# Two-block transformer kernel: gate and up weights of three more expert pairs, and the second block's first projection tiles, taken in halves over k

## The chip, the cores and the metric

The kernel runs on one core of one Trainium2 chip, in float32. The metric is the device time of one execution in microseconds (us), median of the runs. Times below without a unit are microseconds from the start of the profiled span.

## The reference

The input is one sequence of 256 tokens with 1024 features. Two blocks follow one another.

The first block adds a hybrid attention mixer, then a hierarchical mixture of experts: for every token a group of 8 experts is chosen out of 4, and two experts in it. Then it normalises. Each of the 32 experts is a gated network of width 256:

```python
hg = jnp.einsum('nd,edf->nef', t, w_gate)
hu = jnp.einsum('nd,edf->nef', t, w_up)
a = jax.nn.silu(hg) * hu * comb[:, :, None]
y = jnp.einsum('nef,efd->nd', a, w_down)
```

The second block normalises, projects to 3072 columns (`w_in_2`), runs an HGRN2 recurrence on four of the six groups of 512 columns and a convolution with an RG-LRU recurrence on the others, projects out, and ends with a gated feed-forward network of width 2816 and a last normalisation. The columns 2048 to 2559 of `w_in_2` are `lru_x`, the input of the convolution.

## The kernel before

TensorE (PE) does the matrix products, SyncE (SP) issues nearly all weight loads, on one DMA queue, in the order in which its program lists them. All waits are written by hand on semaphores.

**Expert stage.** The 32 experts are worked off as 16 teams of two (experts 2n and 2n+1 are team n). A team has six homes in turn for its weights (`HOMES = 6`, expert e lives in home e % 6): homes 0 to 3 are the slots of the tile `ring`, home 4 is `hs` (with `mixT` for the down weights), home 5 is `tok` and a part of `arena`. So a team's weights can be loaded as soon as the team three places ahead of it has used its own. Per team SP waits for `gate_up_used`, issues gate and up of both experts (`load_gate_up`, 1 MB each, 4 MB together; `load_half` at L572 gives whole matrices with 8 KB a partition, `load_quarter` at L578 gives 0.5 MB pieces with 4 KB a partition for home 5), waits for `chunk_used`, and issues the two down matrices (L599, 1 MB each, rows of 4 KB).

For team n, `next_team(n)` on PE waits for all of its gate and up weights (`weights_there`), then runs `gate_up` (L1218): eight steps over k, in each of them one product for each of the two experts, written as 16 `matmul` calls and seen as 32 instructions. It transposes the activations (L1273), then `down_joined` (L1294) waits for **both** down matrices and multiplies. Products that combine earlier teams (L1303) fill the gaps.

Team 3 (experts 6 and 7) and the last team, 15 (experts 30 and 31), are loaded by halves over k already: `load_last_halves` (L595) sends four 0.5 MB loads with k below 4 and then four with k from 4 on, and `gate_up(..., late=True)` waits for the second four only in front of k = 4. `LATE` says how many loads each weight has on its home's semaphore, and the thresholds `ARRIVED` are added up from it.

**Head of the second block.** Behind the last team's down product PE runs the last combining products (L1313), DVE adds them to the residual `xT` (L2526), and ACT writes `h_raw` in eight tiles (L1903, in the order `JOINED`). PE then makes four tiles of 128 columns out of `h_raw` and the first 512 columns of weight chunk `in2 0` (L1367). Each takes eight steps over k and one PSUM bank of four. The chunk comes in two loads from L660, columns 2048 to 2559 (2 MB) and columns 512 to 767 (1 MB), and PE waits for both in front of the first tile. Behind the second tile PE makes the sum of squares for a normalisation (L1373), behind the third another (L1376). What hangs on L1373 is a chain:

- ACT takes the root (L1908), DVE the reciprocal (L2548), and DVE then scales eight tiles of `hT` (L2551);
- DVE, in program order behind these eight, takes the four finished banks (L2556), and each such copy raises `u2_first` by one;
- PE's fifth tile (L1380) uses the first bank again, and so waits for `u2_first` to be 1, and it reads `hT` too.

```python
                def bank2():
                    u = unit2.up() - 1
                    if u >= 8:
                        pe.wait_ge(u2_taken, u - 3)
                    elif u >= 4:
                        pe.wait_ge(u2_first, u - 3)
                    return ps[:, u % 4, :]
```

Of the kernel before, what the change touches and what calls it, by code (L numbers as in the profile page):

```python
# [94 lines left out]
LATE = ([("expert", e, 4 if e % HOMES == HOMES - 1 or e in (HOMES, HOMES + 1) else 2) for e in range(EXPERTS)]  # L95
        + [("in2", c, 2) for c in range(4)]
        + [("out2", c, 1) for c in range(2)] + [("ffn", c, 2) for c in range(FFN_N)]
        + [("down", c, 1) for c in range(DOWN_N)])
NUMBER = {(kind, c): n for n, (kind, c, _) in enumerate(LATE)}
# [56 lines left out]
def build(nc, x, c, w_ada, b_ada, g_mix, w_in, b_forget, g_out_a, g_out_b, w_out, g_ffn, w_group,  # L156
# [3 lines left out]
    with ExitStack() as ctx:  # L160
# [282 lines left out]
        gu_done, silu_done, act_ready = sem("gu_done"), sem("silu_done"), sem("act_ready")  # L443
        turn_done, turn_taken, y_taken = sem("turn_done"), sem("turn_taken"), sem("y_taken")
        put_done, put_taken, last_halves = sem("put_done"), sem("put_taken"), sem("last_halves")
        w_y_done, w_comb_done = sem("w_y_done"), sem("w_comb_done")
        comb_done, comb_taken = sem("comb_done"), sem("comb_taken")
        parts_ready, h_ready = sem("parts_ready"), sem("h_ready")
# [53 lines left out]
        def _(sp):  # L502
# [77 lines left out]
            def load_gate_up(e):  # L580

                for g in range(2):
                    if e % HOMES <= SLOTS:
                        load_half(e, g)
                    else:
                        for far in range(2):
                            load_quarter(e, g, far)

            def load_last_halves(k_half):
# [50 lines left out]
            for team in range(HOMES // 2, TEAMS):  # L640
                sp.wait_ge(gate_up_used, team - HOMES // 2 + 2)
                if team == HOMES // 2:
                    load_early_halves(1)
                elif team == TEAMS - 1:
                    for k_half in range(2):
                        load_last_halves(k_half)
                else:
                    for e in (2 * team, 2 * team + 1):
                        load_gate_up(e)
                sp.wait_ge(chunk_used, 2 * (team - HOMES // 2) + 2)  # L650
                for e in (2 * team, 2 * team + 1):
                    load_down(e)
            in2 = w_in_2[0].rearrange("(k p) n -> p k n", p=P)
            for ch, parts in enumerate([[(2048, 2560), (512, 768)], [(768, 1024), (0, 512)],
                                        [(1024, 1536), (2560, 2816)], [(2816, 3072), (1536, 2048)]]):
                n = NUMBER["in2", ch]
                free(n)
                w, at = weights("in2", ch, KT, 768), 0
                for lo, hi in parts:
                    sp.dma_start(w[:, :, at:at + hi - lo], in2[:, :, lo:hi]).then_inc(arrived[(n + 2) % SLOTS], 16)  # L660
                    at += hi - lo
# [108 lines left out]
        def _(pe):  # L770
# [439 lines left out]
            def gate_up(n, u, first=False, late=False):  # L1210

                for k in range(KT):
                    if first and k in (0, FIRST_TILES):
                        pe.wait_ge(first_windows, 1 if k == 0 else 2)
                    if late and k == KT // 2:
                        last_halves_there()
                    for h in range(2):
                        last = pe.matmul(ps[WIN * h:WIN * (h + 1), 0, :].rearrange("p (g n) -> p g n", g=2),  # L1218
                                         lhsT=xw[:, u, k, :], rhs=expert_gate_up(2 * n + h, k),
                                         start=k == 0, stop=k == KT - 1)  # L1220
                    if first and k == KT // 2 - 1:
                        last.then_inc(gate_up_used, 1)
# [40 lines left out]
            def weights_there(n):  # L1263
                for e in (2 * n, 2 * n + 1):
                    pe.wait_ge(arrived[e % HOMES], ARRIVED["expert", e])

            def last_halves_there():
                pe.wait_ge(last_halves, 64)

            def turn_act(n):  # L1270

# [68 lines left out]
            def second_block():  # L1340
# [16 lines left out]
                    pe.wait_ge(u2_done, units)  # L1357
                    pe.sem_inc(chunk_used, 1)

                chunk_there("in2", 0)  # L1360
                w = weights("in2", 0, KT, 768)
                for i in range(4):
                    o = bank2()
                    for n, k in enumerate(JOINED):
                        if i == 0:
                            pe.wait_ge(raw_ready, n + 1)
                        last = pe.matmul(o[:, 0:L], lhsT=w[:, k, i * P:(i + 1) * P], rhs=h_raw[:, k, :], start=n == 0,  # L1367
                                         stop=n == KT - 1)
# [269 lines left out]
            with pe.Else():  # L1638
                gather()
                clear_banks()  # L1640
                for team in range(TEAMS):
                    weights_there(team)
                    if team == TEAMS - 1:
                        last_halves_there()
                    with pe.Fori(0, WINDOWS) as w:
                        n = w + team * WINDOWS
                        pe.wait_ge(windows_copied, n + 1)
# [1258 lines left out]
```

## Time and profile before

| | us |
|---|---|
| median of 3 runs | 767.14 |
| lowest and highest | 766.76, 767.94 |
| span of the profiled execution | 762.7 |
| PE busy in it | 730.6 (96%) |
| expert stage's last 4 teams, then second block from | 359.9 to 420.7 |

The page gives the span of the profiled execution, and no other time of it; the median stands 4.4 us above that span, which is what lies around the first and the last instruction. In the lists of the timeline each line is: start, length, engine, line of the program, operation, what it writes and reads, how many; in square brackets the idle time of the engine ahead of it and what ended it. PEld is the weight load that goes with each PE product.

### The profile page before, as it was taken

Reading aid. Unit: us, or ns where it says so; the run is one execution under the profiler, and the core shown is the slowest. Engines: PE = TensorE matmul, PEld = TensorE weight load, DVE = VectorE, ACT = ScalarE, POOL = GpSimd, SP = SyncE. Lnnn points to the kernel's source line nnn. Section 1 sums busy time; section 2 is a strip of 40 time slices with the busy share of each in tenths; the row PEclk is TensorE's granted clock in tenths of the full one; section 3 lists DMA queues with packets and bytes.
Section 4 is the critical chain, followed back from the end, with each engine's and each line's share of the span. In section 5 each row is a group of like instructions: output and inputs, shape, how many; then the busy total and the mean of one; then the engine's idle time right before and its main releaser. Section 6 shows DMA issues by size and latency. Waiting matters only on the chain.

```text
span 762.7 us, 9761 instructions
## 1 busy us (share of the span) xinstructions
PE 730.6 (96%) x3883; PEld 485.9 (64%) x3883; DVE 354.0 (46%) x798; ACT 188.0 (25%) x412; POOL 58.8 (8%) x69
## 2 busy tenths in 40 slices
PE   6999999998889999999989999999999999999996
PEld 4677778786524434343334886788888888885442
DVE  2125666785721212121121876364276656567445
ACT  5014323533511111111011338131321111111002
POOL 3033660040000000000001000000000000000000
PEclk9999999999999999999999999999999999999999
DMA  9998956956999999999999963123454645443401
GB/s 339 339 339 249 396 192 222 354 205 261 351 377 415 416 414 416 418 413 415 419 409 368 371 227 111 46 66 111 151 181 135 197 146 185 157 175 111 165 28 58
DMA packets 78250, 197.27 MB, mean 259 GB/s; under 512 B 3343, under 2 KB 38520, under 8 KB 72312
## 3 DMA queue, kind: packets, MB, share of 16 engines
q1 hardware_dynamic: 77248, 195.37, 68.6%
q10 hardware_dynamic: 664, 0.80, 0.4%
q0 software_dynamic: 288, 0.41, 0.3%
q8 instruction: 33, 0.54, 0.3%
q14 instruction: 17, 0.14, 0.1%
HBM read 195.33 MB, written 1.05 MB: 257 GB/s over the span
## 4 chain that ended last, share of the span: by engine, by line
PE 75%; SPq 10%; DMA 7%; DVE 5%; ACT 1%; issue 1%; POOL 1%; DVEq 0%; ACTq 0%
PE ps L1502 18%; PE ps L1218 9%; PE ps L777 9%; PE ps L1563 9%; PE ps L1294 5%; PE ps L903 4%; PE ps L1127 4%; SPq L572 4%; PE ps L914 2%; DMA arena<-in_w_up 2%; DMA ring<-in_w_ada 2%; SPq L578 2%; PE ps L1089 2%; PE ps L1099 2%; DMA ring<-in_w_in 2%; PE ps L1303 2%
## 5 line engine op out<-in xcount | busy, mean ns | idle before, releaser
L1218 PE MATMUL ps<-ring,arena 128*64 128x512 f32 x352 | 77.6, 593 | 3.1 <-DMA ring<-in_w_up 2.5
L903 PE MATMUL ps<-hs,ring 128*128 128x256 f32 (+1 forms) x288 | 66.2, 384 | 1.0 <-DMA ring<-in_w_in 1.0
L903 PEld LDWEIGHTS ps<-hs,ring 128*128 128x128 f32 (+1 forms) x288 | 52.7, 187 | 12.7 <-issue 3.8
L1218 PEld LDWEIGHTS ps<-ring,arena 128*64 128x64 f32 x352 | 26.3, 137 | 52.5 <-issue 52.5
L2848 DVE SCALAR_TENSOR_TENSOR arena<-arena,own_rows,ps 128x256 f32<-128x256 f32 x16 | 7.7, 480 | 106.8 <-ACT arena L1884 106.8
L777 PE MATMUL ps<-hs,ring 128*128 128x256 f32 x240 | 53.3, 381 | 0.3 <-PE ps L777 0.3
L777 PEld LDWEIGHTS ps<-hs,ring 128*128 128x128 f32 x240 | 45.2, 190 | 7.1 <-issue 0.9
L1502 PE MATMUL ps<-ring,hs 128*128 128x256 f32 x176 | 41.7, 380 | 0.9 <-DVE xT L2727 0.9
L1502 PE MATMUL ps<-ring,mixT 128*128 128x256 f32 x176 | 41.7, 380 | 0.0
L1502 PE MATMUL ps<-arena,mixT 128*128 128x256 f32 x176 | 41.6, 379 | 0.0
L1294 PE MATMUL ps<-ring,arena 128*64 128x512 f32 x176 | 40.2, 598 | 1.0 <-issue 0.5
L1218 PE MATMUL ps<-hs,arena 128*64 128x512 f32 x80 | 35.2, 592 | 2.2 <-DMA arena<-in_w_up 2.2
L1502 PEld LDWEIGHTS ps<-ring,hs 128*128 128x128 f32 x176 | 33.3, 190 | 6.1 <-issue 1.7
L1502 PEld LDWEIGHTS ps<-arena,mixT 128*128 128x128 f32 x176 | 33.4, 190 | 4.5
L1502 PEld LDWEIGHTS ps<-ring,mixT 128*128 128x128 f32 x176 | 32.6, 190 | 4.0
L1884 ACT ACTIVATE arena<-ps 128x256 f32<-128x256 f32 x16 | 6.1, 384 | 108.4 <-PE ps L1218 100.7
L1127 PE MATMUL ps<-mixT,ring 128*128 128x256 f32 x128 | 28.0, 380 | 0.1
L2690 DVE TENSOR_TENSOR arena<-ring 128x1024 f32<-128x1024 f32 x16 | 19.5, 1220 | 15.7 <-PE ps L1563 15.7
L1294 PEld LDWEIGHTS ps<-ring,arena 128*64 128x64 f32 x176 | 11.9, 136 | 23.1 <-issue 22.4
L1127 PEld LDWEIGHTS ps<-mixT,ring 128*128 128x128 f32 x128 | 24.2, 190 | 3.7 <-issue 0.5
L1218 PEld LDWEIGHTS ps<-hs,arena 128*64 128x64 f32 x80 | 10.9, 137 | 24.4 <-issue 24.4
L2856 DVE COPY arena<-ps 64x512 f32<-64x512 f32 x12 | 8.2, 683 | 36.6 <-PE ps L1294 36.6
(483 smaller groups left out, 1215.5 us busy)
## 6 DMA issues: line engine op xcount, KB each, us to landing
ring<-in_w_down SPq DMA_DIRECT2D x23, 1024.0 KB, 18.1
ring<-in_w_gate_up SPq DMA_DIRECT2D x22, 1024.0 KB, 7.2
ring<-in_w_gate SPq DMA_DIRECT2D x18, 1024.0 KB, 17.1
ring<-in_w_up SPq DMA_DIRECT2D x18, 1024.0 KB, 17.9
ring<-in_w_ada SPq DMA_DIRECT2D x5, 3072.0 KB, 12.9
ring<-in_w_down SPq DMA_DIRECT2D x5, 2048.0 KB, 8.1
ring<-in_w_in SPq DMA_DIRECT2D x9, 1024.0 KB, 17.1
ring<-in_w_ada SPq DMA_DIRECT2D x16, 512.0 KB, 9.3
```

Of the source, the lines that this page charges most:

```text
L572: sp.dma_start(dst, src[:, e, :]).then_inc(arrived[e % HOMES], 16)
L578: sp.dma_start(dst, src[:, e, D:2 * D] if far else src[:, e, 0:D]).then_inc(arrived[SLOTS + 1], 16)
L777: last = pe.matmul(o, lhsT=w_of(k), rhs=rhs_of(k), start=k == 0, stop=k == k_n - 1)
L903: last = pe.matmul(o[0:n, 0:L], lhsT=w[:, k, lo:lo + n], rhs=h[:, k, :], start=k == 0, stop=k == KT - 1)
L914: last = pe.matmul(o[:, i * n:(i + 1) * n], lhsT=hT[:, k, b * P:(b + 1) * P], rhs=w[:, k, lo:lo + n], start=k == 0, stop=k == KT - 1 and f ...
L1089: last = pe.matmul(ps[:, m // 2, (m % 2) * L:(m % 2 + 1) * L], lhsT=w[:, k, (m % 4) * P:(m % 4 + 1) * P], rhs=mixT[:, k, :], start=m % 2 = ...
L1127: last = pe.matmul(o, lhsT=w[:, k, (m % 4) * P:(m % 4 + 1) * P], rhs=mixT[:, k, :], start=last_of is None and m % 2 == 0 and k % 4 == 0, s ...
L1218: last = pe.matmul(ps[WIN * h:WIN * (h + 1), 0, :].rearrange("p (g n) -> p g n", g=2), lhsT=xw[:, u, k, :], rhs=expert_gate_up(2 * n + h, ...
L1294: last = pe.matmul(ps[WIN * half:WIN * (half + 1), 2, :], lhsT=act_turned[:, u, at:at + WIN], rhs=expert_down(2 * n + h)[:, k, lo:lo + 512 ...
L1502: last = pe.matmul(o, lhsT=tokens(k), rhs=columns(k), start=start and k == 0, stop=k == 3, skip_group_check=True)
L1563: last = pe.matmul(ps[:, DOWN_BANK[name], :], lhsT=lhsT, rhs=rhs, start=n == 0, stop=n == FT // 2 - 1, skip_group_check=True)
L2690: ve.tensor_tensor(sums[0], lo_2, lo_1, ALU.subtract).then_inc(weight_sums, 1)
```

## The change

Experts 24 to 29, which are teams 12, 13 and 14, are loaded by halves over k like team 15: eight loads of 0.5 MB (4 KB a partition) for a team, the four with k below 4 first. Before, teams 12 and 13 had four loads of 1 MB, and team 14 had two of 1 MB and four of 0.5 MB. The second halves count on semaphores of their own, for which PE waits in front of k = 4.

The chunk `in2 0` is loaded in five pieces instead of two: four of 0.5 MB for the first 512 columns, each over two steps of k, in the order in which PE takes them, and the 1 MB of columns 512 to 767 behind. PE runs the first four k steps of all four tiles, waits for the second pieces, runs the last four k steps of all four tiles, and waits for the 1 MB only then. The two sums of squares stay behind the second and the third tile, which are now behind the second half of these tiles.

```diff
+HALVED = range(24, 30)
+LATE = ([("expert", e, 2 if e in HALVED else 4 if e % HOMES == HOMES - 1 or e in (HOMES, HOMES + 1) else 2) for e in range(EXPERTS)]
+        + [("in2", c, 2 if c else 1) for c in range(4)]
...
+            def load_halves(team):
+                for k_half in range(2):
+                    at = k_half * D
+                    for e in (2 * team, 2 * team + 1):
+                        there = second_half_there[team % (HOMES // 2)] if k_half else arrived[e % HOMES]
+                        for g, src in enumerate((gate_d, up_d)):
...
+                            sp.dma_start(dst, src[:, e, at:at + D]).then_inc(there, 16)
...
+                elif 2 * team in HALVED:
+                    load_halves(team)
...
+                if ch == 0:
+                    for there, k in ((in2_first_k, 0), (in2_first_k, 4), (in2_second_k, 2), (in2_second_k, 6)):
+                        sp.dma_start(w[:, k:k + 2, 0:512], in2[:, k:k + 2, 2048:2560]).then_inc(there, 16)
+                    parts, at = parts[1:], 512
...
+                    if 2 * n in HALVED and k == KT // 2:
+                        second_halves_there(n)
...
-                chunk_there("in2", 0)
                 w = weights("in2", 0, KT, 768)
+                first_banks = [bank2() for _ in range(4)]
+                pe.wait_ge(in2_first_k, 16 + 32)
                 for i in range(4):
-                    o = bank2()
-                    for n, k in enumerate(JOINED):
+                    for n, k in enumerate(JOINED[0:4]):
                         if i == 0:
                             pe.wait_ge(raw_ready, n + 1)
...
+                pe.wait_ge(in2_second_k, 16 + 32)
+                for i in range(4):
+                    for n, k in enumerate(JOINED[4:8]):
...
                     last.then_inc(u2_done, 1)
                     if i == 1:
                         pe.wait_ge(sums_ready, SUMS["g"])
...
+                chunk_there("in2", 0)
                 o = bank2()
```

## Rows read from the trace of the kernel before

**Rows 1.** The page: span, and the first engine of its part 1.

```profile
span 762.7 us, 9761 instructions
PE 730.6 (96%) x3883; PEld 485.9 (64%) x3883; DVE 354.0 (46%) x798; ACT 188.0 (25%) x412; POOL 58.8 (8%) x69
```

**Rows 2.** Timeline of PE, teams 12 to 15 and the head of the second block.

```profile
359.89 7.09 PE L1218 MATMUL ps<-ring,arena 128*64 128x512 f32 x32 [0.67 <-DMA ring<-in_w_up]
...
374.95 7.09 PE L1218 MATMUL ps<-ring,arena 128*64 128x512 f32 x32 [1.80 <-DMA ring<-in_w_up]
...
390.16 0.61 PE L1218 MATMUL ps<-hs,arena 128*64 128x512 f32 x1 [2.16 <-DMA arena<-in_w_up]
...
403.24 7.04 PE L1218 MATMUL ps<-ring,arena 128*64 128x512 f32 x32
...
412.59 3.65 PE L1294 MATMUL ps<-ring,arena 128*64 128x512 f32 x16
...
420.75 7.17 PE L1367 MATMUL ps<-tok,ring 128*128 128x256 f32 x32 [0.52 <-DMA ring<-in_w_in]
```

**Rows 3.** The chain that ended last: team 14's last up load, issue to landing.

```profile
371.72 18.31 DMA arena<-in_w_up
```

**Rows 4.** Busy time by stretch of 5 us; last column GB/s, before it DMA share.

```profile
362.00:367.00 5.00, 5.00 (x25) 1.81 (x21) 0.00 (x0) 0.00 (x0) 0.00 (x0) 1.00 1.03 424
367.00:372.00 5.00, 5.00 (x24) 2.82 (x26) 1.68 (x7) 0.77 (x2) 0.00 (x0) 1.00 1.01 420
...
382.00:387.00 5.00, 4.94 (x27) 2.45 (x28) 1.83 (x7) 1.32 (x4) 0.00 (x0) 1.00 1.01 406
387.00:392.00 5.00, 2.84 (x16) 0.96 (x14) 0.68 (x1) 0.59 (x1) 0.00 (x0) 1.00 1.02 407
...
397.00:402.00 5.00, 5.00 (x26) 2.81 (x26) 1.68 (x7) 0.77 (x2) 0.00 (x0) 1.00 1.03 411
```

**Rows 5.** Loads at L595, one first half and the last second half: issue, landing.

```profile
L595 SPq DMA_DIRECT2D ring<-in_w_up x1: 1076/1076/1076, 384.4 to 384.4; - x1
DMA to landing us min/median/max: 15.8/15.8/15.8
...
L595 SPq DMA_DIRECT2D ring<-in_w_up x1: 3156/3156/3156, 388.4 to 388.4; - x1
DMA to landing us min/median/max: 17.0/17.0/17.0
```

**Rows 6.** Loads at L599 of experts 30 and 31, issued 391.6 and 392.7.

```profile
L599 SPq DMA_DIRECT2D ring<-in_w_down x2: 1076/1638/2200, 391.6 to 392.7; - x2
...
DMA to landing us min/median/max: 16.3/17.9/19.5
```

**Rows 7.** Loads at L660 of chunk in2 0, 2 MB and 1 MB.

```profile
L660 SPq DMA_DIRECT2D ring<-in_w_in x2: 2197/5940/9682, 395.0 to 397.2; - x2
...
DMA to landing us min/median/max: 22.8/23.1/23.5
```

**Rows 8.** Timeline of all engines, head of the second block.

```profile
419.94 3.31 ACT L1903 ACTIVATE tok<-xT,gains 128x256 f32<-128x256 f32 x8 [3.06 <-DVE xT L2526]
...
428.28 0.70 PE L1373 MATMUL ps<-arena,ones 128*128 128x256 f32 x2 [0.35 <-DVE arena L2541]
...
429.02 0.38 ACT L1908 ACTIVATE rstd<-ps 128x256 f32<-128x256 f32 x1 [2.57 <-PE ps L1373]
...
430.46 1.75 DVE L2548 RECIPROCAL rstd<-rstd 128x256 f32<-128x256 f32 x1
...
432.25 3.26 DVE L2551 SCALAR_TENSOR_TENSOR hs<-xT,gains,rstd 128x256 f32<-128x256 f32 x8
...
432.70 3.62 PE L1367 MATMUL ps<-tok,ring 128*128 128x256 f32 x16
...
435.44 0.41 DVE L2556 TENSOR_TENSOR arena<-ps,rstd 128x256 f32<-128x256 f32 x1
...
435.94 1.05 PEld L1380 LDWEIGHTS ps<-hs,ring 128*128 128x128 f32 x5
```

More of the change, by code:

```diff
@@ L94 @@
 FFN_PARTS = {"q": 1, "u": 2, "gate 1": 3, "up 1": 4, "up 0": 5}
-LATE = ([("expert", e, 4 if e % HOMES == HOMES - 1 or e in (HOMES, HOMES + 1) else 2) for e in range(EXPERTS)]
-        + [("in2", c, 2) for c in range(4)]
+HALVED = range(24, 30)
+LATE = ([("expert", e, 2 if e in HALVED else 4 if e % HOMES == HOMES - 1 or e in (HOMES, HOMES + 1) else 2) for e in range(EXPERTS)]
+        + [("in2", c, 2 if c else 1) for c in range(4)]
         + [("out2", c, 1) for c in range(2)] + [("ffn", c, 2) for c in range(FFN_N)]
@@ L445, in build @@
         put_done, put_taken, last_halves = sem("put_done"), sem("put_taken"), sem("last_halves")
+        second_half_there = (last_halves, ada0_there["scale 0"], ada0_there["scale 3"])
+        second_half_before = (0, 16 * 3, 16 * 2)
+        in2_first_k, in2_second_k = in0_first, in0_second
         w_y_done, w_comb_done = sem("w_y_done"), sem("w_comb_done")
@@ L587, in load_gate_up @@
                             load_quarter(e, g, far)
+            def load_halves(team):
[4 more added lines that the diff above has]
+                        for g, src in enumerate((gate_d, up_d)):
+                            h = e % HOMES
+                            if h < SLOTS:
+                                dst = ring[:, h, g * KT * FE + at:g * KT * FE + at + D]
+                            elif h == SLOTS:
+                                dst = hs[:, g].rearrange("p k t -> p (k t)")[:, at:at + D]
+                            else:
+                                dst = far_gate_up[:, g].rearrange("p k n -> p (k n)") if k_half else tok[:, g, :]
+                            sp.dma_start(dst, src[:, e, at:at + D]).then_inc(there, 16)
             def load_last_halves(k_half):
@@ L1265, in weights_there, with second_halves_there @@
                     pe.wait_ge(arrived[e % HOMES], ARRIVED["expert", e])
+            def second_halves_there(n):
+                i = n % (HOMES // 2)
+                teams = sum(m % (HOMES // 2) == i for m in range(HALVED[0] // 2, n + 1))
+                pe.wait_ge(second_half_there[i], second_half_before[i] + 64 * teams)
             def last_halves_there():
-                pe.wait_ge(last_halves, 64)
+                pe.wait_ge(last_halves, 128)
             def turn_act(n):
@@ L1358, in chunk2_used @@
                     pe.sem_inc(chunk_used, 1)
-                chunk_there("in2", 0)
                 w = weights("in2", 0, KT, 768)
+                first_banks = [bank2() for _ in range(4)]
+                pe.wait_ge(in2_first_k, 16 + 32)
                 for i in range(4):
-                    o = bank2()
-                    for n, k in enumerate(JOINED):
+                    for n, k in enumerate(JOINED[0:4]):
                         if i == 0:
                             pe.wait_ge(raw_ready, n + 1)
-                        last = pe.matmul(o[:, 0:L], lhsT=w[:, k, i * P:(i + 1) * P], rhs=h_raw[:, k, :], start=n == 0,
-                                         stop=n == KT - 1)
+                        pe.matmul(first_banks[i][:, 0:L], lhsT=w[:, k, i * P:(i + 1) * P], rhs=h_raw[:, k, :],
+                                  start=n == 0, stop=False)
+                pe.wait_ge(in2_second_k, 16 + 32)
+                for i in range(4):
+                    for n, k in enumerate(JOINED[4:8]):
+                        if i == 0:
+                            pe.wait_ge(raw_ready, n + 5)
+                        last = pe.matmul(first_banks[i][:, 0:L], lhsT=w[:, k, i * P:(i + 1) * P], rhs=h_raw[:, k, :],
+                                         start=False, stop=n == 3)
                     last.then_inc(u2_done, 1)
@@ L1644, in _ @@
                         last_halves_there()
+                    if 2 * team in HALVED:
+                        second_halves_there(team)
                     with pe.Fori(0, WINDOWS) as w:
```

## The prediction

> **What bounds the kernel now.** I read the page first: PE is busy for 730.6 of 762.7 us [rows 1], so a gain must come out of the few places where PE stands still, and whatever delays PE is paid in full. Then I read PE's timeline in the stretch that the change touches [rows 2]. It shows three waits for gate and up weights: 0.67 us ahead of team 12, 1.80 us ahead of team 13, 2.16 us ahead of team 14, together 4.63 us. Team 15, in halves already, starts without a wait, and the second block's first tile waits 0.52 us for its chunk. The chain that ended last runs through team 14's last load, issued at 371.7 and landed at 390.0 [rows 3]: there the DMA stream sets the pace, and not PE.
>
> The third view is the stream itself. In the stretches of 5 us it moves 406 to 424 GB/s with the DMA engines at a share of 1.01 to 1.03 [rows 4]; it is full, and SP has issued far ahead. Its order is fixed, so an earlier PE makes no byte land earlier. The fourth view, issue and landing, gives the stream's milestones: team 15's first halves are there at 384.4 + 15.8 = 400.2, its second halves at 388.4 + 17.0 = 405.4 [rows 5]; the down matrix of expert 30 at 391.6 + 16.3 = 407.9 and that of 31 at 392.7 + 19.5 = 412.2 [rows 6]; the chunk's 2 MB at 395.0 + 22.8 = 417.8 and its 1 MB at 397.2 + 23.5 = 420.7 [rows 7]. PE starts team 15's down product at 412.59 [rows 2]. So PE, which looks free of waits there, is only 0.4 us behind the stream. That is the number that decides about the expert part.
>
> **Team 12 to 14 in halves, taken alone.** A halved team can start 2 MB ahead of its last byte; 2 MB took 405.4 - 400.2 = 5.2 us [rows 5]. A team's products take 7.09 us with their tail, 7.0 us of issue, so 3.5 us a half [rows 2]. PE was ready at 359.22 for team 12, 373.15 for team 13 and 388.00 for team 14 (start less wait). Team 12 then starts at once and gains 0.67; team 13 too, and gains 0.67 + 1.80 = 2.47; team 14 starts its first half at 385.5, is through at 389.0 and waits about 1 us for the last halves. It ends some 3.5 us earlier than now. PE would like to keep these 3.5 us.
>
> **What the smaller rows cost the stream.** The change makes rows of 4 KB out of rows of 8 KB for 10 MB (4 + 4 + 2). The trace holds both kinds: while team 13's whole matrices flow, the rate is 424 and 420 GB/s, while team 14's quarters, down matrices and team 15's halves flow it is 406, 407 and 411 [rows 4]. 10 MB are 10.5e6 bytes: 24.9 us at 422 and 25.7 us at 408, so 0.8 us more. The bounds are 0, if the difference is of the place and not of the rows, and 1.0 us at the extreme pair of these rows (424 and 406 give 1.1). I take 0.8, as the rates follow the kind of load in every one of these rows. The issuing itself costs nothing: SP issues about 15 us ahead of the landing even where it sends the 0.5 MB loads [rows 5], and with thirteen more issues up to the end of this chunk (4, 4, 2, and 3 for the chunk), about 1.1 us each in these rows, it waits for a full queue, not the queue for it.
>
> At this place the Trainium skill speaks against the change: the page "DMA: Bandwidth & Descriptors" (sections "Anatomy of one DMA" and "Bandwidth") gives a fixed 2.0 us to every transfer and wants 1 MiB or more in each. By the formula, if the fixed parts stood in a row, the ten more expert loads would be 20 us; the trace shows that they overlap. The rows that say so: four loads of 0.5 MB landed within 5.2 us of each other, which is their bytes at 403 GB/s and leaves nothing like a fixed part [rows 5].
>
> **What is left of the gain.** With 0.8 us on the stream: team 14's last halves at 390.8, so team 14 ends at 394.4 instead of 397.2 and PE is ready for team 15 at 400.4 instead of 403.24. Team 15's first halves come at 401.0, its second halves at 406.2, so its gate and up end at 409.8 (now 410.3). PE is ready for the down product at 412.1, but the second down matrix lands at 412.2 + 0.8 = 413.0. So the down product starts at about 413.05, which is 0.45 us **later** than now. Nothing of the 3.5 us comes through; the wait has moved to `down_joined` of team 15, and its queue behind it is everything PE has left.
>
> **The chunk in halves.** The first tile starts now at 420.75, because of the 1 MB that it doesn't need. Without that it could start when ACT has written the first tile of `h_raw`, 419.94 + 0.41 = 420.35 [rows 8], so at about 420.4. Its 1 MB of first pieces lies ahead of the present landing at 417.8 and is there. With the 0.45 us the start is at 420.85, 0.1 us later than now.
>
> **The new order of the four tiles.** A tile takes 3.45 us (two in 7.17 with the tail) [rows 2], half a tile 1.72. Now L1373 starts 7.53 us behind the first tile's start, 0.35 of it a wait. In the new order it stands behind six halves: 10.35 us. From there the chain runs on: ACT starts 0.65 us behind (0.63 to 0.74 by how the products pile up), 0.38 for the root, 1.75 for the reciprocal, 3.2 from the first of the eight scalings to the first bank copy, 0.41 for that, 0.1 to the weight load of L1380 [rows 8]. Now the reciprocal starts 1.06 us behind the root's end, because DVE is busy adding squares; later it is free, so 0.05. Sum: 10.35 + 0.65 + 0.38 + 0.05 + 1.75 + 0.05 + 3.2 + 0.41 + 0.1 = 16.94 us from the first tile's start to the fifth tile. PE has work for 4 tiles and two small sums, 14.7 us, and then stands still for 2.3 us. Now this distance is 15.2 us to the weight load at 435.94 and 15.4 to the product, which follows the fourth tile at 432.70 + 3.45 = 436.15. The first bank is taken at 435.85, 0.1 us ahead of the load: the chain has no slack today. The new order costs 16.94 - 15.4 = 1.5 us. This is hard to escape: each term is a duration of this trace, and the one thing that moves is L1373, by 2.8 us less the 1.0 us in which DVE was busy and less the wait.
>
> **The sum.** 0.1 + 1.5 = +1.6 us at the fifth tile. Behind it PE waits almost nowhere in the second block, so the shift reaches the end. DVE's work behind L2556 moves by as much as PE's. 762.7 + 1.6 = 764.3 for the span; with the 4.4 us around it, 768.7 on the median of 767.14. The bounds: with no cost of rows +0.8, and with 1.1 us of it +1.9.
>
> **Rivals.** *The stream's tail catches up.* Expert 31's down matrix lands 4.3 us behind that of 30 though 1 MB is 2.6 us, so some engines lag by 1.7 us [rows 6]. If the shorter rows even this out, the down product starts at 412.1, the first tile at 419.9, and the fifth tile is 0.7 us later than now: 767.8. For it: the lag is not explained. Against: the chunk's own small rows follow it as before.
>
> *The gain comes through* (the other side: faster). One mechanism: the stream does run earlier at its end, so that team 15's halves and expert 31's down matrix don't hold PE, all of the 3.5 us is kept, and the first tile starts 3.4 us ahead of 420.4 at 417.0. Even then the 1.5 us of the new order are paid: 417.0 + 16.94 - 436.15 = -2.2, so 764.9. It decides from the point at which expert 31's down matrix lands ahead of 409.7 (then -1.5). Against: 2.5 us would have to come out of a full stream.
>
> *Every transfer costs a fixed time.* Ten more expert loads hold the stream one by one. By the nearest rows the fixed part is at most 5.2 us less 2 MB at 422 GB/s (4.97), over four loads, 0.06 each; that makes 0.6 us and is no more than my own term. A large one, 0.5 us a load, would give 5 us: 772.
>
> *The halves do nothing for PE,* because the loads in flight land interleaved and the first halves come with the last. Then team 14 ends at 397.9, team 15 at 411.1, the down product starts at 413.4 and the fifth tile is 2.0 us later: 769.2. Against: team 15 didn't wait at all in the kernel before.
>
> **The numbers.** My forecast, 768.7, has 0.55, the catching-up tail 0.2, the gain that comes through 0.1, the interleaved halves 0.1, a large fixed time 0.02; 0.03 is for what I don't see. A measurement of this kernel can tell about 0.2% from no change, 1.5 us. My forecast lies just above that edge, with some 0.6 us of scatter on each side: slower in 0.6 of its cases. With the interleaved halves slower is 0.47, same 0.43, faster 0.10. The range from 765.8 to 770.2 takes in both bounds, the caught-up tail, the interleaved halves and half of the faster case.
>
> **What would show each step.** PE's timeline: the waits at L1218 of teams 12 and 13 gone, one of 1 to 1.7 us inside team 14, one inside team 15, one at L1294 of team 15 until 413.0. The stretches from 350 to 385: about 410 GB/s where it was 420. L1373 some 10.4 us behind the first tile, and a wait of 2.3 us in front of L1380, ended by DVE's L2556. I am wrong if L1294 of team 15 starts ahead of 411.5, or if L1380 follows the fourth tile without a gap.

## The result: 769.03 us, 1.0024 of before

22 runs of the changed kernel have a median of 769.03 us (767.17 to 772.51), 22 runs of the kernel before 767.20 us. The ratio is 1.0024, with a 95% interval of 1.0014 to 1.0034: 1.8 us slower (1.1 to 2.6), where the prediction said 1.6 us slower and 768.7 us.

The span of the profiled execution is 767.7 us and its own time 769.48 us, so 1.8 us lie around the span. (The 4.4 us of the prediction compared the span of one quick execution of before with a median of others. It was taken off and added again, so the forecast of the median doesn't hang on it.) Against the 762.7 us of [rows 1] that is 5.0 us, more than the change is worth. A part of it stands ahead of everything that was changed. These lines are PE's timeline at team 1 in the changed kernel, then the busy time of the stretch (granted clock third from the end):

```profile
214.01 5.35 PE L1327 MATMUL ps<-ring,arena 128*64 128x512 f32 x16 [0.47 <-ACT arena L1932]
```
```profile
215.00:220.00 5.00, 5.00 (x18) 1.55 (x16) 0.60 (x1) 0.59 (x1) 0.00 (x0) 0.69 1.01 391
```

The same 16 products took 3.65 us in the kernel before. The granted clock was 0.69 on the mean of these 5 us, so about 3 us were run at 1.2 GHz instead of 2.4, and PE lost 1.7 us. No such stretch is in the profile of before while PE works. The stream came later in two steps. The second down matrix of team 8 landed at 305.9 instead of 304.5; this may be the fall of the clock, as SP's loads wait for PE up to there, but it isn't taken apart. Team 10 then needed 16.5 us on the stream instead of 15.1, with loads that were not changed and at the full clock; why stays open. Together that is 2.8 us. So traces are compared below by distances inside one trace, counted from a point that lies ahead of the change and belongs to the stream: the landing of team 11's last down matrix. The lines are issue and landing, first the kernel before, then the changed one:

```profile
L599 SPq DMA_DIRECT2D arena<-in_w_down x1: 2509/2509/2509, 329.2 to 329.2; - x1
DMA to landing us min/median/max: 20.6/20.6/20.6
```
```profile
L619 SPq DMA_DIRECT2D arena<-in_w_down x1: 2508/2508/2508, 332.0 to 332.0; - x1
DMA to landing us min/median/max: 20.6/20.6/20.6
```

That is 349.8 and 352.6. I call it the mark. Times of the changed trace have to be lowered by 2.8 us to stand beside those of before. Landings are read to 0.1 us here, so a distance from the mark is no better than that.

### The profile page after: what moved, and what is told of

Read it like the earlier page. It is cut to its first block, busy times and chain, and to the rows that moved or that the text cites. A ratio compares the mean times of both kernels' runs of the same rounds, so it can differ in the third digit from the quotient of the medians.

```text
span 767.7 us, 9775 instructions
## 1 busy us (share of the span) xinstructions
PE 732.8 (95%) x3883; PEld 485.3 (63%) x3883; DVE 355.0 (46%) x798; ACT 187.6 (24%) x412; POOL 58.6 (8%) x69
## 3 DMA queue, kind: packets, MB, share of 16 engines
HBM read 195.33 MB, written 1.05 MB: 256 GB/s over the span
## 4 chain that ended last, share of the span: by engine, by line
PE 79%; DMA 7%; SPq 6%; DVE 4%; issue 1%; POOL 1%; ACT 1%; DVEq 0%; ACTq 0%
PE ps L1543 17%; PE ps L1246 11%; PE ps L803 9%; PE ps L1604 9%; PE ps L1327 6%; PE ps L929 4%; PE ps L1153 4%; DMA ring<-in_w_down 3%; PE ps L940 2%; DMA ring<-in_w_ada 2%; PE ps L1336 2%; PE ps L1115 2%; PE ps L1125 2%; DMA ring<-in_w_in 2%; SPq L538 1%; SPq L615 1%
## 5 line engine op out<-in xcount | busy, mean ns | idle before, releaser
L1246 PE MATMUL ps<-ring,arena 128*64 128x512 f32 x352 | 77.9, 593 | 2.9 <-DMA ring<-in_w_up 2.3
L1327 PE MATMUL ps<-ring,arena 128*64 128x512 f32 x176 | 41.9, 619 | 1.9 <-DMA ring<-in_w_down 0.9
## 6 DMA issues: line engine op xcount, KB each, us to landing
ring<-in_w_in SPq DMA_DIRECT2D x9, 1024.0 KB, 15.8
```

The lines of the kernel that those rows point to most:

```text
L1327: last = pe.matmul(ps[WIN * half:WIN * (half + 1), 2, :], lhsT=act_turned[:, u, at:at + WIN], rhs=expert_down(2 * n + h)[:, k, lo:lo + 512 ...
```

## The profile after

PE's timeline of the changed kernel, teams 13 to 15 and the second block's head, beside [rows 2]:

```profile
378.20 3.65 PE L1246 MATMUL ps<-ring,arena 128*64 128x512 f32 x16 [0.42 <-DMA ring<-in_w_up]
...
388.53 0.61 PE L1246 MATMUL ps<-hs,arena 128*64 128x512 f32 x1 [0.69 <-DMA tok<-in_w_up]
...
393.50 0.64 PE L1246 MATMUL ps<-hs,arena 128*64 128x512 f32 x1 [1.32 <-DMA arena<-in_w_up]
...
403.83 3.65 PE L1246 MATMUL ps<-ring,arena 128*64 128x512 f32 x16 [0.51 <-DMA ring<-in_w_up]
...
408.85 3.65 PE L1246 MATMUL ps<-ring,arena 128*64 128x512 f32 x16 [1.37 <-DMA ring<-in_w_up]
...
415.80 3.65 PE L1327 MATMUL ps<-ring,arena 128*64 128x512 f32 x16 [0.89 <-DMA ring<-in_w_down]
...
423.80 7.14 PE L1400 MATMUL ps<-tok,ring 128*128 128x256 f32 x32 [0.36 <-ACT tok L1946]
...
440.77 3.69 PE L1421 MATMUL ps<-hs,ring 128*128 128x256 f32 x16 [2.06 <-issue]
```

The three waits of before, 4.63 us, have become six: 0.42 inside team 13, 0.69 and 1.32 at the two halves of team 14, 0.51 and 1.37 at those of team 15, 0.89 ahead of its down product. Together 5.20 us: what was gained ahead of team 14 is waited for behind it. The first tile starts 71.20 us behind the mark, before it was 420.75 - 349.8 = 70.95. And a new wait of 2.06 us stands in front of L1421, the fifth tile.

The stream, in the same stretches as [rows 4] and two between (last column GB/s):

```profile
362.00:367.00 5.00, 5.00 (x26) 1.72 (x24) 0.05 (x1) 0.00 (x0) 0.00 (x0) 1.00 1.02 408
367.00:372.00 5.00, 5.00 (x24) 2.62 (x22) 1.67 (x7) 0.77 (x2) 0.00 (x0) 1.00 1.03 410
372.00:377.00 5.00, 5.00 (x26) 1.72 (x24) 0.68 (x1) 0.59 (x1) 0.00 (x0) 1.00 1.03 408
377.00:382.00 5.00, 4.58 (x22) 1.28 (x19) 0.00 (x0) 0.01 (x1) 0.00 (x0) 1.00 1.03 411
```

The stretches of 420 and 424 GB/s are gone; all run at 408 to 411. Two things have changed in these loads, the length of their rows and their number, and the landings tell the two apart. These are the last load of gate and up weights of team 13, first in the kernel before (1 MB, rows of 8 KB), then in the changed one (0.5 MB, rows of 4 KB):

```profile
L572 SPq DMA_DIRECT2D ring<-in_w_up x1: 2118/2118/2118, 351.7 to 351.7; - x1
DMA to landing us min/median/max: 23.1/23.1/23.1
```
```profile
L607 SPq DMA_DIRECT2D ring<-in_w_up x1: 1222/1222/1222, 362.2 to 362.2; - x1
DMA to landing us min/median/max: 16.0/16.0/16.0
```

They land at 374.8 and 378.2. The second down matrix of the team ahead had landed at 364.9 and 367.9, that of team 13 itself lands at 379.9 and 383.3. So before, 4 MB in rows of 8 KB took 9.94 us (to the hundredth in the trace) and the 2 MB of down matrices, two loads of 1 MB in rows of 4 KB, took 5.11 us. In the changed kernel the 4 MB took 10.23 us in pieces of 0.5 MB, and the down matrices 5.13. With rows of 4 KB a MB costs 2.56 us, in loads of 1 MB and of 0.5 MB alike; with rows of 8 KB it costs 2.49. The number of transfers costs nothing that shows here. (The down matrices are another tensor; that difference is left.)

Issue and landing at the end of the stream, beside [rows 5] (last second half of team 15) and [rows 6] (the down matrices of experts 30 and 31):

```profile
L615 SPq DMA_DIRECT2D ring<-in_w_up x1: 1241/1241/1241, 393.5 to 393.5; - x1
DMA to landing us min/median/max: 15.3/15.3/15.3
...
L619 SPq DMA_DIRECT2D ring<-in_w_down x2: 1089/1640/2190, 394.8 to 395.9; - x2
...
DMA to landing us min/median/max: 18.3/19.0/19.8
```

They land at 408.8, 413.1 and 415.7. Behind the mark that is 56.2, 60.5 and 63.1 us; before, 405.4, 407.9 and 412.2 less 349.8 are 55.6, 58.1 and 62.4. So the matrix that PE waits for is 0.7 us later.

The head of the second block, all engines, beside [rows 8]:

```profile
434.24 0.59 PE L1413 MATMUL ps<-arena,ones 128*128 128x256 f32 x2
...
434.87 0.38 ACT L1951 ACTIVATE rstd<-ps 128x256 f32<-128x256 f32 x1 [5.23 <-PE ps L1413]
435.29 1.75 DVE L2591 RECIPROCAL rstd<-rstd 128x256 f32<-128x256 f32 x1 [1.54 <-ACT rstd L1951]
...
437.07 3.25 DVE L2594 SCALAR_TENSOR_TENSOR hs<-xT,gains,rstd 128x256 f32<-128x256 f32 x8
...
440.27 0.41 DVE L2599 TENSOR_TENSOR arena<-ps,rstd 128x256 f32<-128x256 f32 x1
...
440.74 3.32 PEld L1421 LDWEIGHTS ps<-hs,ring 128*128 128x128 f32 x16 [2.43 <-issue]
```

The sum of squares stands 10.44 us behind the first tile instead of 7.53. DVE is idle when the root is done, the reciprocal follows at once, the eight scalings, then the copy of the first bank, whose end at 440.68 releases the fifth tile. PE's own work was done 2.06 us ahead of the fifth tile's start.

## The experiments

In the table the first tile is counted from the mark (in the same trace), and the seventh tile (the one that starts behind a gap of 0.30 us in every one of these kernels) from the first tile. Both are read in one profiled execution each; the ratio is of many runs. It isn't the quotient of the medians, from which it differs by up to 0.6 us in these experiments.

The last column is an estimate from the runs' times and mean clocks. The 103 executions of before that stand beside the experiments, in three sets, show how time goes with the clock: a line through them, each set around its own mean, gives 0.60 us more for every thousandth of mean granted clock less, and it takes up 0.65 of the variance. The column is the mean of a kernel's runs less the mean of before beside them, brought to the same clock by that line, in us, with two standard errors of the means. For the change itself the clocks of before are not on record. What the clock does is taken up in the last section.

| kernel | ratio to before, 95% | first tile | seventh tile | sum | at equal clock, us |
|---|---|---|---|---|---|
| before | 1 | 70.95 | 22.78 | 93.73 | 0 |
| the change | 1.0024 (1.0014 to 1.0034) | 71.20 | 24.43 | 95.63 | - |
| experts only | 0.9989 (0.9976 to 1.0002) | 71.67 | 22.58 | 94.25 | +0.1 ± 0.4 |
| chunk only | 1.0022 (1.0010 to 1.0035) | 70.86 | 24.43 | 95.29 | +1.2 ± 0.5 |
| sum early | 1.0003 (0.9991 to 1.0016) | 71.17 | 22.93 | 94.10 | 0.0 ± 0.6 |
| rows only | 1.0023 (1.0011 to 1.0036) | 73.21 | 22.92 | 96.13 | +0.4 ± 0.7 |
| more rows | 1.0025 (1.0009 to 1.0041) | 71.15 | 24.42 | 95.57 | +2.1 ± 0.7 |
| split down | 1.0003 (0.9986 to 1.0019) | 70.46 | 24.43 | 94.89 | +0.4 ± 0.6 |
| old order, late 1 MB | 0.9994 (0.9978 to 1.0010) | 70.80 | 22.92 | 93.72 | 0.0 ± 0.4 |
| filled waits | 0.9971 (0.9956 to 0.9986) | 70.79 | 22.93 | 93.72 | -0.5 ± 0.4 |
| all together | 0.9985 (0.9975 to 0.9995) | 70.27 | 22.93 | 93.20 | -0.5 ± 0.5 |
| fifth tile's wait filled | 1.0033 (1.0020 to 1.0047) | 71.09 | 24.42 | 95.51 | +2.1 ± 1.0 |
| team 14 alone, filled | 0.9995 (0.9984 to 1.0005) | 69.75 | 22.93 | 92.68 | -0.9 ± 0.6 |
| filled waits, late 1 MB | 1.0012 (0.9999 to 1.0026) | 70.82 | 22.93 | 93.75 | +0.2 ± 0.8 |

The ratios stray from the traces' sums by up to 2.2 us (0.7 in the middle). At equal clock nine of the twelve experiments agree with their trace within the two errors, if 1.7 us are taken off "rows only" for a fall of the clock in its own profile; "experts only" and "filled waits" miss by little, "split down" by 0.8 us.

**Experts only.** The chunk `in2 0` as before.

```diff
-        + [("in2", c, 2 if c else 1) for c in range(4)]
+        + [("in2", c, 2) for c in range(4)]
...
-                if ch == 0:
-                    for there, k in ((in2_first_k, 0), ...
...
+                chunk_there("in2", 0)
                 for i in range(4):
-                    for n, k in enumerate(JOINED[0:4]):
+                    for n, k in enumerate(JOINED):
```

> Experts 24 to 29 in halves as in the changed kernel; the chunk in2 0 is loaded, waited for and used as before. My theory: the stream comes 0.8 us later from the 4 KB rows, PE's 3.5 us are taken away by the waits of team 15, and the chunk's 1 MB lands at 421.5 instead of 420.7, so +0.8 us against before (768.0). L1373 stands 7.5 us behind the first tile, no wait in front of the fifth tile. Rival, the gain of PE comes through: -0.3 us or better. Rival, the expert halves cost what the whole change costs: +1.9 us.

Its timeline of PE from team 14's second half on:

```profile
391.13 0.64 PE L1242 MATMUL ps<-hs,arena 128*64 128x512 f32 x1 [1.35 <-DMA arena<-in_w_up]
...
406.50 3.65 PE L1242 MATMUL ps<-ring,arena 128*64 128x512 f32 x16 [1.38 <-DMA ring<-in_w_up]
...
413.50 3.65 PE L1323 MATMUL ps<-ring,arena 128*64 128x512 f32 x16 [0.97 <-DMA ring<-in_w_down]
...
421.86 7.17 PE L1396 MATMUL ps<-tok,ring 128*128 128x256 f32 x32 [0.71 <-DMA ring<-in_w_in]
...
429.19 0.70 PE L1402 MATMUL ps<-arena,ones 128*128 128x256 f32 x2 [0.16 <-DVE arena L2572]
```

In the trace everything is where I had put it: the mark is at 350.2, the first tile 0.7 us later than before, waiting for the chunk's 1 MB at the end of a stream that is 0.7 us late. The seventh tile is 0.5 us late, since the wait for the sum shrank. But the runs are 0.9 us faster than before by the ratio (from 1.8 faster to 0.2 slower) and 0.55 us by the medians, where I had said 0.8 slower. Their mean clock was higher, 0.9976 against 0.9966; at equal clock 0.1 us slower is left. "Rows only" and the section on the clock take this up.

**Chunk only.** The experts as before (`HALVED = range(0, 0)`), the rest of the change kept.

> No expert in halves beyond those of before; the chunk in2 0 in five pieces and the four tiles in the new order, as in the changed kernel. My theory: the first tile starts 0.3 us earlier (420.4), the sum of squares stands 10.35 us behind it instead of 7.5, the fifth tile 16.9 us behind it instead of 15.4: +1.2 us against before (768.4). PE waits 2 to 2.3 us in front of the fifth tile. Rival, the order costs nothing because the waits are hidden: -0.3 us.

```profile
423.01 7.15 PE L1400 MATMUL ps<-tok,ring 128*128 128x256 f32 x32 [0.36 <-ACT tok L1946]
...
439.99 3.69 PE L1421 MATMUL ps<-hs,ring 128*128 128x256 f32 x16 [2.06 <-issue]
```

1.7 us slower by the ratio, 1.56 us by the trace, 1.2 us expected. The first tile waits for ACT and no longer for the load, but this gain is only 0.1 us behind the mark, and the new order takes 24.43 instead of 22.78 us. Nearly the whole loss of the change is in this part.

**Sum early.** The changed kernel with another order on PE, nothing else (`half_tiles(tiles, half)` runs four k steps of these tiles):

```diff
+                half_tiles((0, 1), 0)
                 pe.wait_ge(in2_second_k, 16 + 32)
                 for i in range(4):
...
+                    if i == 2:
+                        half_tiles((2, 3), 0)
+                    last = half_tiles((i,), 1)
                     last.then_inc(u2_done, 1)
                     if i == 1:
                         pe.wait_ge(sums_ready, SUMS["g"])
```

> The changed kernel, but PE takes both halves of tiles 0 and 1 first, then the sum of squares L1373, then both halves of tiles 2 and 3. All loads and waits on loads stay. My theory: the sum is back at 7.5 us behind the first tile, the fifth tile at 15.4 us, the wait of 2.1 us in front of it is gone: 1.5 us faster than the changed kernel, +0.1 to +0.4 us against before. Rival, the wait in front of the fifth tile has another cause (the chunk's 1 MB, or the code of PE): no change against the changed kernel, 1.0024 of before.

```profile
422.88 7.15 PE L1403 MATMUL ps<-tok,ring 128*128 128x256 f32 x32 [0.35 <-ACT tok L1950]
...
430.57 0.70 PE L1417 MATMUL ps<-arena,ones 128*128 128x256 f32 x2 [0.54 <-DVE arena L2588]
...
445.81 7.14 PE L803 MATMUL ps<-hs,ring 128*128 128x256 f32 x32 [0.30 <-PE ps L803]
```

The sum is 7.69 us behind the first tile, the wait in front of the fifth tile is gone, the seventh tile stands at 22.93 instead of 24.43: 1.5 us. By the ratios 1.0024 became 1.0003, 1.6 us. This shows where the change loses: in the place of L1413 in PE's program.

**Rows only.** As "experts only", but PE waits for the second halves ahead of k = 0.

```diff
-                    if 2 * n in HALVED and k == KT // 2:
+                    if 2 * n in HALVED and k == 0:
                         second_halves_there(n)
```

> As the run with only the experts in halves, but PE waits for the second halves ahead of k = 0 already, so it has the smaller rows and none of the earlier starts. My theory: PE waits 1 to 3 us in one piece in front of teams 12, 13 and 14, team 14 starts 0.8 us later than before, the down product of team 15 too, and the end is +0.8 us against before: the same as with the earlier starts, since the stream decides. Rival, the halves are worth something to PE: this run is 1 us or more slower than the one with only the experts in halves.

1.8 us slower than before by the ratio, and 2.6 us slower than "experts only"; by the medians of the same runs it is 1.2 and 1.7 us. I had expected no difference between the two. The trace gives one reason, in team 14 and in the stretch around it (granted clock third from the end):

```profile
390.84 0.64 PE L1242 MATMUL ps<-hs,arena 128*64 128x512 f32 x1 [2.25 <-DMA arena<-in_w_up]
...
391.29 1.04 PE L1242 MATMUL ps<-hs,arena 128*64 128x512 f32 x1
```
```profile
385.00:390.00 5.00, 3.59 (x17) 1.00 (x16) 1.80 (x7) 0.71 (x2) 0.00 (x0) 1.00 1.03 411
390.00:395.00 5.00, 4.16 (x12) 1.62 (x14) 0.00 (x0) 0.00 (x0) 0.00 (x0) 0.66 1.02 409
```

Behind a wait of 2.25 us the products of 593 ns take 1040: PE runs at 1.2 GHz for some 3.4 us, and team 14's products take 8.7 us instead of 7.0. Of the 2.3 us by which the first tile is late, this is 1.7; the rest, 0.6, is the late stream. The stream itself is as in "experts only": mark at 349.8, last load of team 14 40.9 us behind it (before 40.2). Without the 1.7 us the sum would be 94.4, beside 94.3 of "experts only": in the trace the earlier starts are worth nothing at the end, as expected. The difference of the runs is for the most part one of the clock, 0.9952 against 0.9976. At equal clock 0.3 us of it are left, which is within the errors.

**More rows.** Experts 18 to 29 in halves (`HALVED = range(18, 30)`).

> The changed kernel with experts 18 to 29 in halves instead of 24 to 29: 10 MB more in rows of 4 KB. My theory, the smaller rows cost the stream 0.08 us a MB: the down matrix of expert 31 lands 0.8 us later against the stream's own start than in the changed kernel, and the kernel is 0.8 us slower than the changed one (1.0034 of before). Rival, the later end of the stream has to do with the last teams alone: as the changed kernel, 1.0024.

The ratio is 1.0025, beside 1.0024 of the changed kernel; the interval (0.0016 to each side) holds both 1.0024 and the expected 1.0034. The mark lies within the changed rows here, so its sum of 95.57 lacks what teams 9 to 11 cost. Between the second down matrices of teams 8 and 9, and of 9 and 10, the stream needs 15.4 us each, where it needs 15.1 in the kernel before: 0.3 us for each team of 4 MB, as expected. Team 11 is no witness, 15.8 us against 15.2: the changed kernel shows at team 10, with whole matrices, that a single team can be later by more than that (16.5). So the cost of the rows shows in the stream, and whether it reaches the end stays open.

**Split down.** The changed kernel with a later wait:

```diff
                 for h in range(2):
                     pe.wait_ge(down_there[(2 * n + h) % HOMES], DOWN_THERE[2 * n + h])
-                for h in range(2):
                     for k in range(2):
```

> The changed kernel, but the down product waits for the second expert's down matrix only behind the first expert's products (1.8 us later), in all teams. My theory, PE's gain dies at the wait for expert 31's down matrix: team 15's down product starts 0.9 us earlier against the stream and the kernel is 0.9 us faster than the changed one (1.0012 of before). Rival, the gain is gone already at team 15's halves: no change against the changed kernel.

```profile
407.17 3.65 PE L1246 MATMUL ps<-ring,arena 128*64 128x512 f32 x16 [1.38 <-DMA ring<-in_w_up]
...
421.15 7.14 PE L1399 MATMUL ps<-tok,ring 128*128 128x256 f32 x32 [0.36 <-ACT tok L1945]
```

The wait at the down product is gone and the first tile stands 70.46 us behind the mark, 0.74 earlier than in the changed kernel (expected 0.9). The ratio went from 1.0024 to 1.0003, 1.6 us, with intervals that overlap. The place where PE's gain is lost last is this wait; the 1.38 us inside team 15 is the one ahead of it.

**Old order, late 1 MB.** The kernel before, but the chunk comes in five pieces and the 1 MB of columns 512 to 767 is waited for in front of the fifth tile only. PE's part, against the kernel before:

```diff
-                chunk_there("in2", 0)
+                pe.wait_ge(in2_first_k, 16 + 32)
+                pe.wait_ge(in2_second_k, 16 + 32)
...
+                chunk_there("in2", 0)
                 o = bank2()
```

> The kernel before, but the chunk in2 0 comes in five pieces and PE waits for the 1 MB of columns 512 to 767 only in front of the fifth tile; order of the tiles and sums and the experts' loads as before. My theory: first tile at 420.4 instead of 420.75, nothing lost behind it: -0.3 us (0.9996). Rival, the pieces themselves cost something: +0.3 us or more.

The ratio says nothing here (0.9978 to 1.0010). The trace does: the first tile is 0.15 us earlier, the seventh 0.14 us later behind it, the sum is the same 93.7. PE waits 0.54 instead of 0.35 us for the squares in front of the sum, for they depend on the experts' result and not on the tiles. So an earlier first tile wins nothing, even without the new order.

**Filled waits.** The kernel before with two products more:

```diff
                 pe.wait_ge(windows_copied, n + 1)
+                if n in (TEAMS - 3, TEAMS - 2):
+                    for _ in range(2):
+                        pe.matmul(ps[:, 0, :], lhsT=ones[:], rhs=xT[:, 0:2, :].rearrange("p k t -> p (k t)"), start=True,
+                                  stop=True)
                 weights_there(n)
```

> The kernel before with two added products of 512 columns (1.7 us, result overwritten) ahead of the wait for the weights of team 13 and of team 14, where PE stands still for 1.8 and 2.2 us. It tells whether the earlier starts are worth time through the clock. Theory A, such a standstill lets the granted clock fall to 1.2 GHz for some 3 us in a part of the executions (seen in the profile of the run with the smaller rows alone: 0.66 in 390 to 395): mean clock of the runs up by 0.001 and the median 0.5 us or more below before. Theory B, the clock has nothing to do with these waits: median +0.0 to +0.2 us, clock as before.

2.2 us faster than before (1.1 to 3.4), with the trace's distances unchanged at 93.72. The mean granted clock over the 12 runs was 0.9977, over the 35 runs of before beside them 0.9959. Both are as theory A had it, but the last experiment doesn't bear it out, and in the traces the falls of the clock stand elsewhere (see the last section).

**All together.** Experts 24 to 29 in halves, the split wait, the old order, the late 1 MB.

> The changed kernel's experts in halves, the down product waiting for its second expert only in front of that expert's products, the tile order and the sums as before, and the chunk's 1 MB waited for in front of the fifth tile. My theory: of the changed kernel's +1.9 us the new order's 1.5 us go and the wait for expert 31's down matrix goes (0.9 us); by the terms it is 0.5 us faster than before, and 1 us faster if the shorter standstills keep the clock up as in the run with the experts alone (0.9987 to 0.9993). Rival, the wait moves on to the first pieces of the chunk: no better than 1.0.

0.9985, the interval wholly below 1: 1.2 us faster than before. The trace gives 0.5 of it (93.20), as the terms had said, and so do the runs at equal clock.

**Fifth tile's wait filled.** The changed kernel with two products of 512 columns into an idle bank behind the fourth tile.

> The changed kernel with two added products of 512 columns (1.7 us, result unused) behind the fourth tile, where PE stands still for 2.06 us in front of the fifth. They can't move the fifth tile earlier. Theory A, this standstill too lets the clock fall in a part of the executions: mean clock above the changed kernel's 0.9958 and the median 0.5 us or more below the changed kernel's (1.0015 of before or less). Theory B, the whole cost of the new order is the standstill itself: 1.0024 of before, as the changed kernel.

```profile
438.83 3.69 PE L1424 MATMUL ps<-hs,ring 128*128 128x256 f32 x16 [0.34 <-issue]
```

The wait is 0.34 instead of 2.06 us, the seventh tile is where it was (24.42), and the ratio is 1.0033, not lower than 1.0024. Filling this wait brings nothing; whether the products add something can't be told from the intervals.

**Team 14 alone, filled.** Only experts 28 and 29 in halves, the split wait, the old order, the late 1 MB, and the two products ahead of team 13.

> Only experts 28 and 29 in halves (2 MB in smaller rows, 0.15 us on the stream), the later wait for the second down matrix, tile order as before, the 1 MB waited for in front of the fifth tile, and two added products in the 1.8 us wait of team 13. By the terms: team 14 ends 2.1 us earlier, team 15's second halves let 1.1 us of it through, the down product no less, the first tile at 419.3: 1.4 us faster than before from the starts, and some 0.5 us more from the clock: 0.9975 to 0.9982. Rival, it is the clock alone that counts: as the run with the added products, 0.9971, or no better than 0.9990 if team 14's shorter wait was the one that mattered.

The trace gives the best sum of all, 92.68, 1.05 us ahead of before: 1.4 had been expected, 0.3 of it from the late 1 MB, which is worth nothing. The ratio, 0.9995 (0.9984 to 1.0005), shows less, and lies outside the 0.9975 to 0.9982 that I had named; the mean clock was 0.9962, in the runs of before beside it 0.9968.

**Filled waits, late 1 MB.** The kernel before with the added products of "filled waits" and the late 1 MB of "old order".

> The kernel before with the added products ahead of the waits of teams 13 and 14 and the chunk's 1 MB waited for in front of the fifth tile: the two runs 0.9971 and 0.9994 together. If they add up 0.9965; if the first was an outlier of its session, 0.9985.

1.0012, above both values that I had named. With the added products in the same place as in "filled waits" the mean clock was 0.9959 (before beside it 0.9968), and the 0.9971 did not come back.

## Why the prediction was right, point by point

*The stream gets slower by the 4 KB rows, 0.8 us.* Held: 408 to 411 GB/s where it was 420 to 424, the last load of team 14 and expert 31's down matrix both some 0.7 us later behind the mark. "Rows only" and "experts only" show the same with the chunk left alone (team 14's last load 40.9 us behind the mark in both, against 40.2). That it is the rows, and not the number of transfers, is shown by the down matrices of 1 MB, which cost as much for each MB as the pieces of 0.5 MB. The prediction gives its upper bound once as 1.0 and once as 1.1 us; the rows give 1.1.

*PE's 3.5 us are lost to the halves and the down matrix of team 15.* Held: waits of 0.51, 1.37 and 0.89 us where the prediction's milestones give 0.6, 1.7 and 0.9. Team 15's down product starts at 415.80 less 2.8, so at 413.0, where it had 413.05. Taking the last of the waits away moved the first tile by 0.74 us.

*The first tile starts 0.1 us later.* 0.25 us: the same sum, with a small miss.

*The new order costs 1.5 us.* The fifth tile starts 440.77 - 423.80 = 16.97 us behind the first, where the chain of terms gave 16.94; PE's wait is 2.06 us where I had 2.3: the prediction counted PE's work by the starts of its products, and the wait is counted from the end of the last one. "Sum early" gives back 1.50 us. The seventh tile is 1.65 us further behind the first than before. The other 0.15 us is lost in the old order too once the first tile no longer waits for the 1 MB, as PE then waits 0.54 instead of 0.35 us for the squares ("old order, late 1 MB").

*The sum.* +1.9 us at the seventh tile, +1.8 us by the runs, +1.6 us predicted. That the runs come within 0.2 us is in part luck: their interval alone is 1.1 to 2.6 us, and the ratios of the experiments stray further from their traces. What carries the prediction are the terms above. The one thing that it had wrong was the span: 764.3 predicted, 767.7 seen. I had taken the profiled execution of before for a typical one. Over 35 executions of before that stood beside the first four experiments the spans have a median of 765.1, and the 762.7 is one of the quickest.

*The rivals.* The tail doesn't catch up, though it does even out: experts 30 and 31's down matrices land 2.6 us apart instead of 4.3. But the first came later rather than the second earlier, so it brought nothing. A fixed cost of transfers in a row is excluded by the stream's rate: 0.5 MB loads and 1 MB loads with the same rows cost the same for each MB. (The two sections of the Trainium skill's page "DMA: Bandwidth & Descriptors" that the prediction names give their figures for loads issued from GpSimd; here SP issues them.) The interleaved halves would have given 769.2, nearer to the measured 769.03 than the forecast; only the trace tells them apart. Team 14 starts its first half at 388.53 less 2.8, so at 385.7, and ends at 394.3 instead of 397.2, so its first halves did come ahead of the last ones. The gain that comes through to the end was excluded by the trace; in the runs with the experts alone there is some gain against the terms, which leads to the clock.

## What to carry to other kernels

Where a stream of loads is full up to a certain byte, starting the consumers earlier moves the wait to the last load in it; ask which landing PE is nearest to, not which wait is longest, and see whether that wait can be put behind a part of the work. When tiles are worked in halves over k, everything that hangs behind a finished tile (here a sum of squares, and through ACT and DVE the release of a bank) moves back too: keep the product that starts the longest chain at its old distance. And compare two profiles by distances from a mark ahead of the change, as one execution can differ from another by more than the change.

## What the runs showed of the hardware that I had not expected

Single short falls of the granted clock. In 9 of the 14 profiles of this case one stretch of 3.4 us was run at 1.2 GHz. It begins at 188.6 to 189.4 in four of them, at 213.8 to 215.0 in four, and at 391.3 in "rows only", each time at most 2 us behind the end of a standstill of PE: one of 1.50 us that ends at 187, one of 1.23 us that ends at 213, one of 2.25 us. In the two that are shown it cost PE 1.7 us each.

The length of the standstill doesn't decide. The first two stand in all 14 profiles with the same length (1.50, and 1.23 to 1.25 us), and in none of them did the clock fall behind both. Here is the one at 213 in the kernel before, where it did not fall, and then in the changed kernel, where it did:

```profile
212.76 0.44 PE L1273 MATMUL ps<-ident,arena 128*128 128x128 f32 x2 [1.23 <-DVE arena L2848]
```
```profile
213.09 0.44 PE L1306 MATMUL ps<-ident,arena 128*128 128x128 f32 x2 [1.23 <-DVE arena L2891]
```

It is an affair of the execution. In the kernel before, over the 35 executions beside the first four experiments, the six with a mean clock of 0.999 took 765.96 us on average, the five with 0.994 took 768.51. That is about 0.5 us for each thousandth of mean clock (0.60 by the line through all 103), and it makes most of the scatter of the runs.

By this the odd ratios can be read. "Experts only" had a mean clock of 0.9976 over its runs, before 0.9966, "rows only" 0.9952, and at equal clock the three lie within 0.4 us of each other. Does the kernel set its own clock, because PE stands still in one piece ahead of teams 13 and 14 for at most 1.35 us in "experts only" and for 2.25 us in "rows only"? That isn't shown, and there is something against it: in eight of the nine profiles with a fall it lies at 189 or 214, ahead of every load and every product that the change or the added products touch (only the split wait reaches back to there). The added products in the same waits came with a clock of 0.9977 once and 0.9959 the other time, and filling the fifth tile's wait changed nothing. What decides in an execution whether the clock falls stays open.
